# A hybrid decoder step on one Trainium2 core: page numbers read ahead of the wait, x reloaded in pieces

## What is computed

```python
# u = x @ w_in, split into cq, ckv, kr, z, xBC, dt, mq, g
# branch A: latent attention; branch B: Mamba-2; branch M: cross-attention into 256 memory tokens
ckv_past   = cache_ckv[page_table].reshape(bs, past, KV_LORA)     # 8 x 16 pages of 128 keys x 256
krope_past = cache_krope[page_table].reshape(bs, past, ROPE_DIM)  # and x 64
s_past = q_lat @ ckv_past + q_rope @ krope_past
p = softmax([s_past, s_new]);  o = p @ [ckv_past, ckv_new]
o_mem = softmax(mq @ cache_mem_k) @ cache_mem_v                   # per batch: 256 x 4 heads x 256
m = sig(gA)*(o_mla@w_o_mla) + sig(gB)*(o_ssm@w_o_ssm) + sig(gM)*(o_mem@w_o_mem)
x1 = LN(alpha*x + m@w_out);  y = LN(alpha*x1 + relu(x1@w_up+b_up)^2 @ w_down + b_down)
```

## Time and profile before

| | us |
|---|---|
| median of 3 runs | 1699.37 |
| lowest and highest of them | 1696.22, 1700.43 |
| the profiled execution, device time | 1697.17 |
| its span in the trace (first to last instruction) | 1694.5 |
| PE busy | 1630.6 (96%) |
| mean granted TensorE clock, share of full speed | 0.984 |

### The profile page before, as it was taken

The page is one execution under the profiler, slowest core; times in us unless marked ns, Lnnn a source line. Parts: engine busy times, 40 slices in busy tenths (PEclk is TensorE's granted clock), DMA queues, the critical chain, the costliest instruction groups (busy, mean ns, idle before and its releaser), DMA issues.

```text
span 1694.5 us, 27030 instructions
## 1 busy us (share of the span) xinstructions
PE 1630.6 (96%) x10950; PEld 1412.6 (83%) x10950; DVE 781.0 (46%) x1350; ACT 453.2 (27%) x857; POOL 406.8 (24%) x344
## 2 busy tenths in 40 slices
PE   8999999999999999999989879999997999999995
PEld 6878787787878888888777667789997999999995
DVE  5667677775343222233223222344478760177334
ACT  2252433435332222222212110142225111111122
POOL 0041221404020000001333200114435443344332
PEclk9999999999999999999999989999998999999998
DMA  5424233252362222225877765332221222222321
GB/s 182 162 79 161 87 125 125 95 182 81 100 226 75 66 73 75 75 63 194 250 248 228 239 265 199 141 130 92 88 87 51 88 88 88 88 88 88 88 63 53
DMA packets 70846, 210.62 MB, mean 124 GB/s; under 512 B 10210, under 2 KB 26851, under 8 KB 65731
## 3 DMA queue, kind: packets, MB, share of 16 engines
q1 hardware_dynamic: 50816, 155.99, 28.3%
q10 hardware_dynamic: 13762, 31.93, 5.3%
q0 software_dynamic: 6144, 20.98, 4.0%
HBM read 194.01 MB, written 14.86 MB: 123 GB/s over the span
## 4 chain that ended last, share of the span: by engine, by line
PE 80%; DVE 6%; issue 5%; DMA 4%; POOLq 2%; ACT 1%; POOL 1%; SPq 0%; DVEq 0%; ACTq 0%
PE acc L1891 29%; PE acc L1824 21%; PE acc L1837 7%; PE acc L2197 3%; PE acc L2160 3%; POOLq L519 2%; DMA work<-in_page_cols 2%; PE acc L2143 2%; POOL work L524 1%; PE bank L2251 1%; DMA ring<-in_stream 1%; PE bank L2211 1%; PE bank L2230 1%; PE bank L2212 1%; DVE work L1292 1%
## 5 line engine op out<-in xcount | busy, mean ns | idle before, releaser
L1824 PE MATMUL acc<-xt,ring 128*128 128x272 f32 x1504 | 358.9, 395 | 0.0
L1824 PEld LDWEIGHTS acc<-xt,ring 128*128 128x128 f32 x1504 | 282.4, 190 | 67.7 <-issue 12.0
L1891 PE MATMUL acc<-x_parts,f_parts 128*128 128x272 f32 x1408 | 219.6, 291 | 10.7 <-DVE x_parts L1219 6.1
L546 POOL TENSOR_TENSOR f_parts<-ring,f_parts 128x1024 fp32r<-128x1024 f32 x65 | 158.4, 2437 | 247.3 <-ACT f_parts L753 247.1
L1891 PEld LDWEIGHTS acc<-x_parts,f_parts 128*128 128x128 f32 x1408 | 196.0, 191 | 13.4 <-issue 6.0
L524 POOL DMA_DIRECT2D work<-in_page_cols x128 | 68.9, 538 | 445.9 <-PE bank L2251 345.7
L1891 PE MATMUL acc<-f_parts 128*128 128x272 f32 x1344 | 172.3, 289 | 0.0
L1891 PEld LDWEIGHTS acc<-f_parts 128*128 128x128 f32 x1344 | 170.4, 188 | 0.1
L1837 PE MATMUL acc<-work_high,high 128*128 128x272 f32 x464 | 138.5, 299 | 0.0
L1837 PE MATMUL acc<-work_high,ring_low 128*128 128x272 f32 x464 | 133.9, 289 | 0.0
L753 ACT ACTIVATE f_parts<-ring 128x1024 fp32r<-128x1024 f32 x65 | 68.8, 1059 | 239.2 <-PE acc L1891 204.5
(11 more groups left out here) (369 smaller groups left out, 2519.2 us busy)
## 6 DMA issues: line engine op xcount, KB each, us to landing
ring<-in_stream SPq DMA_DIRECT2D x216, 512.0 KB, 3.6
work<-in_page_cols POOLq DMA_DIRECT2D x128, 160.0 KB, 3.4
attended<-in_ssm_state ACTq DMA_DIRECT2D x8, 1024.0 KB, 6.8
work<-cum_rows SPq DMA_DIRECT2D x32, 256.0 KB, 4.6
out_ssm_s<-attended ACTq DMA_DIRECT2D x8, 1024.0 KB, 5.6
work<-in_ckv_rows ACTq DMA_DIRECT2D x64, 128.0 KB, 4.0
work<-in_ckv_rows SPq DMA_DIRECT2D x64, 128.0 KB, 3.4
work<-in_memk_cols SPq DMA_DIRECT2D x8, 1024.0 KB, 6.7
```

Of the source, the lines that this page charges most:

```text
L546: pool.tensor_tensor(lo, ring[:, s * BLOCK:(s + 1) * BLOCK], hi.bitcast(F), SUB).then_inc(sem["split_ready"], 1)
L1824: m = pe.matmul(acc[p][:, half, 0:width], w[:, k * P:(k + 1) * P], x(kk)[:, half * width:(half + 1) * width], start=kk == 0, stop=kk == n_ ...
L1891: m = pe.matmul(acc_half, w[:, k * P:(k + 1) * P], x[:, kk, of], start=kk == 0 and n == 0, stop=kk == last and n == 2)
```

## The change

On POOL, the 16 page numbers of a batch are read in one go at the head of the batch's turn of the loop, before the first wait for `keys_used`; the waits and the 16 DMAs follow with the numbers in registers. Nothing is computed otherwise, and the count of instructions is the same. On SP, the one load of x becomes eight loads of one chunk each (128 x 544, 0.28 MB), put between the cached memories from `(3)` to `(13)`, and the first three stream blocks are issued between cached memories `(0)` to `(3)` instead of behind x. The two waits on x now want all eight landings.

```diff
@@ POOL
             for b in range(DEC_BATCH):
+                ids = [pool.value_load(page_ids[0:1, bass.ds(b * N_PAGES + i, 1)], min_val=0, max_val=N_POOL - 1)
+                       for i in range(N_PAGES)]
                 for kq in range(4):
+                    pool.wait_ge(sem["keys_used"], b * 4 + (kq + 1))
                     for i in range(4):
-                        p = pool.value_load(page_ids[0:1, bass.ds(b * N_PAGES + (kq * 4 + i), 1)],
-                                            min_val=0, max_val=N_POOL - 1)
-                        if i == 0:
-
-                            pool.wait_ge(sem["keys_used"], b * 4 + (kq + 1))
                         pool.dma_start(keys[kq][:, i * KEYS_W:(i + 1) * KEYS_W],
-                                       page_cols[p]).then_inc(sem[f"keys_in_slot{kq}"], 16)
+                                       page_cols[ids[kq * 4 + i]]).then_inc(sem[f"keys_in_slot{kq}"], 16)
@@ SP
-            for n in range(4):
-                cached_mem(n)
-            sp.dma_start(X, x_t).then_inc(sem["x0_loaded"], 16)
-            load(3)
+            def load_x(*cs):
+                for c in cs:
+                    sp.dma_start(X[:, c, :], x_t[:, c, :]).then_inc(sem["x0_loaded"], 16)
+            cached_mem(0)
+            load()
+            cached_mem(1), cached_mem(2)
+            load()
+            cached_mem(3)
+            load()
+            load_x(0)
             cached_mem(4), cached_mem(5)
             load()
+            load_x(1, 2)
             cached_mem(6), cached_mem(7)
             load(2)
+            load_x(3)
             cached_mem(8), cached_mem(9)
             load()
+            load_x(4)
             cached_mem(10), cached_mem(11)
             load(2)
+            load_x(5)
             cached_mem(12), cached_mem(13)
             load()
+            load_x(6, 7)
             cached_mem(14), cached_mem(15)
@@ ACT, and the same on PE
-            act.wait_ge(sem["x0_loaded"], 32 + 16)
+            act.wait_ge(sem["x0_loaded"], 32 + KC * 16)
```

More of the change, by code:

```diff
@@ L2397, in _ @@
                     cached_mem_values((5, 6, 7))
-            pe.wait_ge(sem["x0_loaded"], 32 + 16)
+            pe.wait_ge(sem["x0_loaded"], 32 + KC * 16)
             project(0, of_x)
```

## The result

| | before | after |
|---|---|---|
| median, us | 1699.59 (4 runs) | 1672.00 (4 runs) |
| lowest and highest | 1696.22, 1700.43 | 1671.12, 1672.79 |
| ratio to before, 95% interval | | 0.9841 (0.9824 to 0.9858) |
| profiled execution, device time | 1697.17 | 1671.78 |
| its span | 1694.5 | 1669.7 |

The changed kernel is faster by 1.6%, 27.6 us; 1673 was forecast. In the code of after the turns' lines have new numbers: L2258 and L2262 score the keys (L2247 and L2251 before), L2275 turns the probabilities (L2264), L1848 is the split product (L1837), L1037 the gate on ACT (L1026), L2326 the memory scores (L2315), L2368 the sample values (L2357), L1835 the plain product (L1824).

What follows compares the result with a forecast made beforehand. PE, 96% busy, was taken as the bound, with late keys costing 22.3 us. Gains of 16.6 (turns) and 8.7 (stream block) made 25.3 us, giving 1671.9 from the profiled execution and 1674.1 from the median; forecast 1673, range 1667 to 1686.

Steps and rivals of the forecast that it cites:

- The step: POOL, between two page DMA starts: 0.60 us instead of 1.15, with bounds 0.54 (descriptor work) and 1.06 (dispatch waits).
- The reads ahead: POOL, first batch: the 16 reads delay the first page by 8.3 us from 472.3 us, at no cost.
- Keys 19 us after L2258: Key pages for PE: all there 3.4 + 9.8 + 6 = 19 us after the key scoring starts.
- The next wait: PE at L2264: waits some 0.6 us for ACT's exponentials; turn 24.3 us, gain 16.6 us over seven turns.
- The stream block: Memory part: block M0 lands 4 to 6 us after issue, L1824 starts at about 1003.7; gain 8.7 us with clock.
- The term that was mis-sized: First L1824 on PE: 1.5 us from full clock, since the idle before it shrinks to about 0.6 us.
- The sum: Whole kernel: 16.6 + 8.7 = 25.3 us, so 1669.2 of span and 1671.9 of device time.
- The covers: SP's later loads: x, wanted at 1115.09, and cached_mem(3), about 9 us later, still arrive in time.
- A step of 1.06 or more: POOL's burst: step stays at 1.06, POOL paces the turns, only 3 to 5 us there; about 1686; chance 0.12.
- a step that grows in a dense burst: POOL's burst: descriptors wait for room or port, step over 1.15 us; at 1.3, 1715 us; chance 0.03.
- That the clock falls in the turns: PE after L2247: 1.2 GHz after 0.7 us of idle, about 1.5 us a turn, up to 10; 1683; chance 0.08.
- the first of the two rules: POOL's page DMAs: starved by VectorE's shared port, about 3.1 us instead of 0.62; kept as a small-chance rival's mechanism.

Runs made afterwards that it cites:

- e4: The changed kernel with one more, unused page-number read on POOL ahead of each page DMA: 1698.57 us, ratio 0.9992.
- e3: The changed kernel with ACT rounding the next block before it issues its 8 row DMAs: 1666.96 us, ratio 0.9793.
- e10: The changed kernel with the sample-copy wait moved between the halves of the first L1835 and every narrow L2368 product made twice: 1677.10 us.
- e7: The changed kernel with the four cached memories ahead of the three stream blocks, x still behind them in pieces: 1673.99 us, ratio 0.9843.
- e6: The changed kernel with x in one load of 2.2 MB in the place of its first eighth: 1672.52 us, ratio 0.9836.
- e2: The kernel before with only SP's new list, POOL's reads left in the burst: 1692.26 us, ratio 0.9946.
- e5: The changed kernel with one more, unused page-number read on POOL ahead of every second page DMA: 1673.42 us, ratio 0.984.
- e9: The changed kernel, ACT rounding before its row DMAs, sample-copy wait between the first L1835's halves, memory-values wait moved from ahead of L2326 behind it: 1663.21 us.
- e1: The kernel before with only POOL's page numbers read ahead of the wait, SP's list as before: 1680.03 us, ratio 0.9875.

## Why the prediction was right, step by step

- **The step.** Forecast 0.60 us between bounds 0.54 and 1.06; measured 0.59. A page's dispatch does run beside the descriptor work of the one before: 0.50 and 0.54 us of work fit into a step of 0.59. The choice between the bounds came out right, but its ground was thinner than the prediction has it. These are the rows of before for the one long DMA (POOL: start, us, idle before):

```profile
472.33 0.71 POOL L524 DMA_DIRECT2D work<-in_page_cols  x1 [21.20 <-issue]
473.51 0.54 POOL L524 DMA_DIRECT2D work<-in_page_cols  x1 [0.47 <-issue]
```

  The next one starts 1.18 us later. Had the dispatch to wait for POOL, the step would have been 0.02 + 0.71 + 0.50 = 1.23: since a read hides part of the delay, the two bounds differ here by 0.08 us and not by 0.17, in a single case that came out 0.03 over the usual 1.15. That it pointed the right way is partly luck. e4, at a step of 1.14, shows what a step beyond 0.92 costs.
- **The reads ahead.** They delay the first page from 472.3 to 480.2 us, 7.9 us (8.3 forecast), and nobody wanted it. In the turns they lie in POOL's idle time.
- **Keys 19 us after L2258.** The first page starts 3.4 us after it (855.99 to 859.42), the last one 9.7 us later (867.29 and three steps), and 5.1 us is the median landing: some 18.2, worked out, not read from one row. PE wants them 24 us after.
- **The next wait.** Forecast 0.6 us at L2264 (now L2275) in seven turns for ACT's exponentials, a turn of 24.3 us, gain 16.6. Measured 0.56, 24.18, 17.4. The chain was 13.63 us long (13.60 forecast). e3 shows that it, and nothing else, held the rest.
- **The stream block.** Forecast landing 4 to 6 us after issue; measured 3.6. Start 0.6 us behind L2357 (now L2368), measured 0.52. **The term that was mis-sized** is the clock: the prediction took 1.5 us for the first L1824 back at full speed, 7.5 us long, because the idle before it would shrink. It took 9.29. The step took idle time for the only reason that the clock was low there. e10, and e3 and e7 with the 32 products of before, show that it can fall in the narrow products of L2357 (now L2368) ahead of any idle time behind them. The gain was 7.1 us instead of 8.7. In e6's execution, where the clock held, the stretch from the last gate to the product's end took 987.58 + 7.60 - 974.85 = 20.3 us, a gain of 8.8. So the term differs from one execution to another, and the prediction's value came in 1 of the 7 profiles with this wait of 0.52 us.
- **The sum.** 25.3 us of span forecast, 24.8 measured: 0.8 too little in the turns, 1.6 too much in the memory part. That these errors partly cancel is luck. Against the medians the changed kernel came out 1.0 us below the forecast. The profiled execution of before lies under its median, and the prediction counted that by half. The granted clocks of the runs (e2) suggest that this distance was a matter of how often the clock fell in the turns, and the change took those falls away; subtracting from the profiled execution (1671.9) would then have been the better choice, and it is nearer.
- **The covers.** x: the last piece is issued at 1067.0, no piece took more than 8.1 us, and it is wanted at 1090.23; 15 us to spare. `cached_mem(3)` and the second block behind a PE wait made no new wait.
- **The rivals.** A step of 1.06 or more was wrong, and so was a step that grows in a dense burst: POOL's DMAs took 0.536 to 0.707 us, as before. That the clock falls in the turns behind L2275's wait or L2258's narrow products didn't happen there, 1.00 in all of them, but it did at L2368, whose products have another form (128*128 with 32 columns; L2258's are 128*32 with 256).

On the first of the two rules that the prediction weighed, the dense burst tells something, but less than a test. In this window of after, with columns PE, PEld, DVE, ACT and POOL busy, DVE worked for half of the time, and 16 page DMAs took their usual time on POOL:

```profile
787.60:797.90 10.30, 10.30 (x82) 9.67 (x81) 5.23 (x19) 3.44 (x8) 8.61 (x16) 1.00 0.98 337
```

8.61 / 16 = 0.54 us each. The Trainium skill, "SBUF — State Buffer", section "SBUF: two separate sides", has POOL's descriptors held up while VectorE runs an operation in a 2-port perf mode, and names a float32 copy from SBUF to SBUF as one. No such copy lies in this window: DVE's only copy there reads from `bank`, and the rest are subtractions, maxima, sums and small operations of at most 1.23 us. Which of them run in that mode the profile does not say. So no run here shows the case that the page describes, and the window doesn't speak against it; what holds for this kernel is that none of its 128 page DMAs took POOL over 0.707 us.

## What to carry to other kernels

Where an engine reads an index and then issues a DMA by it, and has to wait for a buffer first, read all indices ahead of the wait: each read costs the sequencer 0.55 us, and behind the wait 15 of the 16 stood on the path. Look then for what is late next before booking the idle time as gain: 22.3 us were lost to late keys, 17.4 came back at once, and the rest only when the issue of 8 other DMAs had left the front of a chain. A block that is needed soon should not stand in a queue behind megabytes that are needed late; whether these come in one piece or eight did not matter.

## What the runs showed of the hardware

- The granted clock can fall while the matrix engine is busy without a gap: in the row of e10, 64 products of 32 columns, PE busy 9.01 of 9.01 us, clock 0.77. The weights' loads were just as busy (9.01). With 32 such products it was 0.90 in e3 and 1.00 in after.
- Behind the same 0.52 us of idle time and the same products, one execution kept clock 1.00 (L1829 of e6, 7.60 us), another had less (L1835 of after, 9.29 us; the same product in e5, 10.64). Such a product has no one duration: 1.6 to 3.0 us of it change from one execution to another.
- The spread of the runs does not tell which state such a product is in: e9, in whose profile it is fast, spreads over 1.1 us where after spreads over 3.1 and before over 7.1 on the same chip, but e1, in whose profile it is slow (9.01 us), spreads over 0.9.
- POOL's step is what its sequencer does, added up: 0.59 us for a dispatch, 0.55 more for a value read between (1.14 in e4). The DMA's 0.54 us of descriptor work runs beside it and shows in neither.
